# Full-size products of constants between the samples' small products, in one kernel of a decoder trunk

## The chip, the cores and the metric

The kernel runs on one core of one Trainium2 chip. The metric is the device time of a launch in microseconds. Before the change it is 3067.97 us, the median of three runs (3066.2 to 3071.03).

## What is computed

One layer of a hybrid decoder for two groups that share the weights: a prompt of 2048 tokens and 8 samples of 4 new tokens each, model width 1024. The layer is: RMS norm, one projection, three parallel head groups (A, windowed attention; B, dilated attention; C, an RWKV-7 recurrence of 6 heads of 64), output projection and residual, RMS norm, squared-ReLU MLP of width 4096 and residual, final norm. Everything is computed in f32, partly in sums of rounded halves.

The change lies in group C. Cut to what matters:

```
def wkv_scan(s0, r, w, k, v, kk, a):
    # S_t = S_{t-1} diag(w_t) + (S_{t-1}(-kk_t)) (kk_t*a_t)^T + v_t k_t^T ;  y_t = S_t r_t
    ...

def rwkv_mixer(zc, z_before, s0, w):
    z_prev = shifted by one token
    zs = zc + (z_prev - zc) * c_mu
    r, k, v, zw, za, zg = split(zs)
    decay = exp(-exp(-softplus(-(c_w0 + tanh(zw) @ c_w2)) - 0.5))
    a = sigmoid(c_a0 + za @ c_a2);  g = sigmoid(zg) @ c_g2
    kk = heads(k * c_k_k) / its norm over a head;  k = k * (1 + (a - 1) * c_k_a)
    y, s_fin = wkv_scan(s0, ...)
    y = norm of y over a head, * c_ln_w + c_ln_b, + sum(r * k * c_r_k) * v
    return y * g, s_fin
```

The prompt starts from a zero state, each sample from a state of its own (`state_c_wkv`).

## The kernel before

`decoder_trunk` (line 3366) calls the stages one after the other: `project`, `prompt_attention`, `rwkv` for the prompt (names `cp_...`, with the samples' attention as a side job), `rwkv` for the samples (`cs_...`), `out_project`, `mlp`. Each stage is a block of five engine programs with a barrier at its end. `project`, `out_project` and `mlp` are dense products of 128x128 weights.

`rwkv` (line 1543) writes the recurrence in chunks. For the prompt a segment is 256 tokens, in four chunks of 64, taken two at a time as a group. For the samples there is one segment, one group and one chunk, which holds all 32 tokens, four of each sample. All products are small: a product of one head takes 64 or 32 rows and columns of the 128x128 array, and the two heads of a pair lie in different halves of it. Each f32 product is two records in the trace.

The order of work is written out by hand. `walk` calls the same steps for each engine's program:

- `prepare(seg, i)`, `i` from 0 to 10: gates, decay, key norm. TensorE makes `w_pre`, `a_pre`, `g_pre`, `kksum` (i = 1 to 4), `kback` (i = 7, line 1722) and `bonus` (i = 9, line 1728). For the samples, `state_queries` stands here and there between them: the first state times `r`, 8 samples one after the other, products of 4 columns (line 1674).
- `levels_of`: the chunk's own matrices (`gab` and `m`, lines 1819 and 1826), their transposes `tok` (line 1841), one head of `state_rows` (line 1665), and then the inverse by doubling, in five levels for the prompt and one for the samples (`yl` line 1855, `dtt` line 1869).
- `hop`, prompt only: from chunk to chunk, `rhs`, `u` and then state and output `y` (lines 1778 to 1800), with a ScalarE copy after each. Those of the last group of the last segment have nothing left to stand between and follow one another.
- `special`, samples only: two state queries, the other five heads of `state_rows` (80 records), `rhs` (1881), `u` (1886), output (1892 and 1893).
- `finish(seg, i)`: mean (line 1743), variance (1749), its inverse spread back over the heads (1755). For the samples the twelve `update` products of the final state (line 1685, 512 columns) stand between these, one, one and ten; then VectorE adds and scales the state (2187, 2192) and SyncE stores it.

The engines wait for one another by counted semaphores: `E.done(product, name, seg)` on TensorE, `W_` where a result is needed. Each engine takes its instructions in the order written.

`keep_busy` (line 70) issues full-size products of the constant `hones` (128x128) into a bank that nobody reads. There are such products in both recurrences: 16 before the samples' first wait, some behind `prepare` 1 to 3, and 24 at the very end (`last_fill` 8); in the samples they go to `q[4]`, which `u` uses too. In the samples' stage ScalarE (`ahead.high`, lines 2499 and 2490) and VectorE (`ahead.low`, 2505 and 2495) also prepare the weights and the first two tiles of the output projection: ScalarE in `prepare` 6 to 9, ahead of `levels_of`; VectorE two pieces in `levels_of`, three in `special`, three in `finish` 9.

The results of `prepare` and `finish` go into `pb`, a view of four quarters of 256 columns, which is two banks of PSUM.

## Time and profile before

| | |
|---|---|
| median of three runs | 3067.97 us |
| the profiled execution | 3062.81 us |
| its span, first to last instruction | 3061.0 us |
| TensorE busy | 2921.0 us, 95% |
| VectorE, ScalarE, GpSimd busy | 2162.6, 944.7, 317.9 us |
| mean granted clock of TensorE | 0.981 |
| samples' recurrence, first instruction to the next stage's first product | 1418.67 to 1484.48 us |

The granted clock is the share of full speed (2.4 GHz) that TensorE was given; it has two levels here, 1.00 and 0.50. The table by stretches gives it for any stretch. In a timeline a row is a run of like instructions on one engine: start, time from the first's start to the last's end, engine, line, what is written and read, shape, count; in brackets the engine's idle time before it and what ended that. The end of a product is modelled, so the start of the next run says better how long one took.

### The profile page before, as it was taken

Reading aid. Unit: us, or ns where it says so; the run is one execution under the profiler, and the core shown is the slowest. Engines: PE = TensorE matmul, PEld = TensorE weight load, DVE = VectorE, ACT = ScalarE, POOL = GpSimd, SP = SyncE. Lnnn points to the kernel's source line nnn. Section 1 sums busy time; section 2 is a strip of 40 time slices with the busy share of each in tenths; the row PEclk is TensorE's granted clock in tenths of the full one; section 3 lists DMA queues with packets and bytes.
Section 4 is the critical chain, followed back from the end, with each engine's and each line's share of the span. In section 5 each row is a group of like instructions: output and inputs, shape, how many; then the busy total and the mean of one; then the engine's idle time right before and its main releaser. Section 6 shows DMA issues by size and latency. Waiting matters only on the chain. (4 is left out here: it accounts for less than half of the span.)

```text
span 3061.0 us, 65513 instructions
## 1 busy us (share of the span) xinstructions
PE 2921.0 (95%) x27757; PEld 2556.3 (84%) x27757; DVE 2162.6 (71%) x3708; ACT 944.7 (31%) x1414; POOL 317.9 (10%) x453
## 2 busy tenths in 40 slices
PE   8999999999888998898999999999999999999998
PEld 6899998566777877787787999999998888888886
DVE  4789885776566666654346999999997666666667
ACT  5533332655332333322133323323331111111013
POOL 0000000643232322330000000000000000000000
PEclk9999999999999999997899999999999999999999
DMA  7644443441222330002365533433436222212212
GB/s 230 206 128 164 139 139 110 143 122 56 73 94 89 105 110 28 23 8 83 115 189 183 185 124 137 173 123 135 166 126 243 70 70 70 84 56 84 70 56 112
DMA packets 182275, 353.48 MB, mean 115 GB/s; under 512 B 27776, under 2 KB 115968, under 8 KB 171488
## 3 DMA queue, kind: packets, MB, share of 16 engines
q1 hardware_dynamic: 181984, 349.29, 34.4%
q8 instruction: 220, 3.60, 0.5%
q14 instruction: 71, 0.58, 0.1%
HBM read 254.65 MB, written 94.60 MB: 114 GB/s over the span
## 5 line engine op out<-in xcount | busy, mean ns | idle before, releaser
L2960 PE MATMUL m_bank<-m_hh,m_wuh 128*128 128x348 f32 (+1 forms) x1344 | 431.5, 321 | 6.1 <-DVE m_wul L3196 4.6
L2961 PE MATMUL m_bank<-m_hl,m_wuh 128*128 128x348 f32 (+1 forms) x1344 | 429.4, 319 | 0.0
L3272 DVE TENSOR_TENSOR m_y_low<-m_y_low,m_bank 128x512 f32<-128x512 f32 x320 | 216.7, 686 | 152.5 <-PE m_bank L2962 149.8
L289 PE MATMUL p_bank<-p_hl,p_wh 128*128 128x348 f32 (+1 forms) x840 | 269.7, 321 | 0.0
L288 PE MATMUL p_bank<-p_hh,p_wh 128*128 128x348 f32 (+1 forms) x840 | 269.4, 321 | 0.0
L2960 PEld LDWEIGHTS m_bank<-m_hh,m_wuh 128*128 128x128 f32 x1344 | 253.0, 188 | 8.3 <-DVE m_wul L3196 5.2
L2961 PEld LDWEIGHTS m_bank<-m_hl,m_wuh 128*128 128x128 f32 x1344 | 253.4, 189 | 0.0
L2962 PE MATMUL m_bank<-m_hh,m_wsl 128*128 128x348 f32 (+1 forms) x768 | 246.3, 321 | 0.0
L2962 PE MATMUL m_bank<-m_wuh,m_wul 128*128 128x512 f32 x512 | 199.2, 389 | 0.0
L3214 DVE TENSOR_TENSOR m_stage<-m_stage,m_bank 128x348 f32<-128x348 f32 (+1 forms) x336 | 166.1, 512 | 45.6 <-PE m_bank L2962 40.6
L3272 DVE TENSOR_TENSOR m_mix<-m_mix,m_bank 128x512 f32<-128x512 f32 x192 | 130.1, 686 | 92.9 <-PE m_bank L2962 92.8
L2962 PE MATMUL m_bank<-m_hh,m_wul 128*128 128x348 f32 (+1 forms) x576 | 184.7, 321 | 0.0
L288 PEld LDWEIGHTS p_bank<-p_hh,p_wh 128*128 128x128 f32 x840 | 157.8, 188 | 0.1
L289 PEld LDWEIGHTS p_bank<-p_hl,p_wh 128*128 128x128 f32 x840 | 157.8, 188 | 0.0
L3066 ACT ACTIVATE m_wuh<-m_wur 128x1536 fp32r<-128x1536 f32 x47 | 70.1, 1491 | 279.4 <-PE m_bank L2962 279.4
L290 PE MATMUL p_bank<-p_hh,p_wsl 128*128 128x348 f32 (+1 forms) x480 | 153.9, 321 | 0.0
L558 DVE TENSOR_TENSOR p_stage<-p_stage,p_bank 128x348 f32<-128x348 f32 (+1 forms) x210 | 103.2, 512 | 62.5 <-PE p_bank L290 60.1
L2962 PEld LDWEIGHTS m_bank<-m_hh,m_wsl 128*128 128x128 f32 x768 | 144.7, 188 | 0.0
L2960 PE MATMUL m_bank<-m_wd,m_wsl 128*128 128x512 f32 x352 | 137.7, 391 | 0.0
L2961 PE MATMUL m_bank<-m_wd,m_wsl 128*128 128x512 f32 x352 | 137.0, 389 | 0.0
L2157 DVE TENSOR_TENSOR cp_Tm<-cp_Tm,cp_q 128x384 f32<-128x384 f32 x64 | 35.4, 554 | 142.7 <-PE cp_q L1865 71.8
L3070 ACT ACTIVATE m_wuh<-m_wsr 128x2048 fp32r<-128x2048 f32 x47 | 90.2, 1920 | 118.1 <-DVE m_wsr L3176 118.1
(477 smaller groups left out, 7194.4 us busy)
## 6 DMA issues: line engine op xcount, KB each, us to landing
m_wur<-w_up SPq DMA_DIRECT2D x48, 1024.0 KB, 5.3
p_war<-w_fm SPq DMA_DIRECT2D x30, 1024.0 KB, 6.3
m_wur<-uT SPq DMA_DIRECT2D x24, 1024.0 KB, 5.3
p_ring<-units SPq DMA_DIRECT2D x30, 768.0 KB, 5.8
uT<-m_stage SPq DMA_DIRECT2D x64, 348.0 KB, 4.9
out_projT<-p_stage SPq DMA_DIRECT2D x40, 348.0 KB, 6.7
cp_z<-out_projT SPq DMA_DIRECT2D x8, 1408.0 KB, 7.8
uT<-m_stage SPq DMA_DIRECT2D x32, 344.0 KB, 4.2
```

The lines of the kernel that those rows point to most:

```text
L288: pe.matmul(out, wh_, mh, start=first, stop=False)
L289: pe.matmul(out, wh_, ml, start=False, stop=False)
L290: return pe.matmul(out, wl_, mh, start=False, stop=last)
L558: dve.tensor_tensor(keep(q, to, n), keep(q, of, n), pbank(q, p, n), ALU.add).then_inc(joined, 1)
L2157: i = e.tensor_tensor(Tm[sl], Tm[sl], packed(1, sl), ALU.add)
L2960: pe.matmul(out, wh_, mh, start=first, stop=False)
L2961: pe.matmul(out, wh_, ml, start=False, stop=False)
L2962: return pe.matmul(out, wl_, mh, start=False, stop=last)
L3066: act.activation(wslot(wh[q % 2], A11, 3), wslot(wa[q % 3][0], 1, 3), ACT.Copy).then_inc(w_high, 1)
L3070: act.activation(wslot(wh[q % 2], S1, 4), ws[q % 2][0][:, :], ACT.Copy).then_inc(w_high, 1)
L3214: dve.tensor_tensor(keep(q, to, n)[:, 0, :], keep(q, of, n)[:, 0, :], pbank(q, p, n), ALU.add).then_inc(joined, 1)
L3272: dve.tensor_tensor(yh, yh, db[b % ND][:, :], ALU.add).then_inc(y_added, 1)
```

## The change

A bank of its own is made for the filling products of the samples: `pb` becomes 96 columns in a row in the first of its two banks, and `idle_bank` is in the second. `fill(n)` writes there in the samples' stage, and elsewhere into the bank `q[at]`. `last_fill` becomes a call of `fill`; its counts stay. New calls:

- samples: one behind each head of `state_rows` and of `state_queries`, one after every second update product but the last, two behind `gab`, one behind each `tok`, three behind `yl`, one behind `dtt`, three behind `rhs`, three behind `u`, two behind the output, and in `prepare` two behind `i = 4` and one behind `i = 7`;
- prompt: in the last group of the last segment two behind `u` of both chunks and two behind `rhs` of the second chunk, into `q[2]`.

Nothing waits for the new products; they stand in TensorE's order.

```
@@ -1598,7 +1598,8 @@
         S1 = s.sb(n_("S1"), [P, NP3, nb, HD])
         q = [s.ps(n_(f"q{i}"), [P, 512]) for i in range(6 if sample else 5)]
         pbanks = s.ps(n_("pb"), [P, 4, 256])
-        pb = pbanks[:, 0:NP3, 0:W]
+        pb = pbanks[:, 0, 0:NP3 * W].rearrange("p (a w) -> p a w", a=NP3) if sample else pbanks[:, 0:NP3, 0:W]
+        idle_bank = pbanks[:, 2, 0:P]
         c_in, z_in = own_.c_in, own_.z_in
         n_consts = own_.n_consts
         stored = s.sem(n_("stored"))
...
@@ -1656,6 +1657,10 @@
         def tensor_walk(e):
             W_ = lambda st, name, seg: st.wait(e, name, seg)
 
+            def fill(n, at=4):
+                if not isinstance(e, Rehearsal):
+                    keep_busy(e, idle_bank if sample else q[at][:, 0:P], hones[:, :], hones[:, :], n)
+
             def heads(n):
                 return [(p, h) for p in range(n) for h in range(2)]
 
...
@@ -1664,6 +1669,7 @@
                     for b in range(NB):
                         e.matmul(q[3][rows(h), p * HD:(p + 1) * HD], am[half(h), p, b, :], S0[half(h), 0, p, b, :],
                                  start=(p == 0 and b == 0), stop=False)
+                    fill(1)
 
             queries = heads(NP3)
 
...
@@ -1673,6 +1679,7 @@
                     for b in range(NB):
                         e.matmul(y_bank(half(h), p, NQ * b, NQ), S0[half(h), 0, p, b, :],
                                  ar_[0][half(h), p, 0, 1, NQ * b:NQ * (b + 1)], start=(p == 0 and b == 0), stop=False)
+                    fill(1)
 
             updates = [(name, t_, p, h) for t_, name in ((1, "vm"), (0, "um")) for p, h in heads(NP3)] if sample else []
 
...
@@ -1686,10 +1693,8 @@
                                   start=(name == "vm"), stop=(name == "um"))
                     if not updates:
                         E.done(mm, ("s", 0), 0)
-
-            def fill(n):
-                if not isinstance(e, Rehearsal):
-                    keep_busy(e, q[4][:, 0:P], hones[:, :], hones[:, :], n)
+                    elif len(updates) % 2 == 0:
+                        fill(1)
 
             def prepare(seg, i):
                 zs = zs_[seg % NPAR]
...
@@ -1730,11 +1735,7 @@
                     if sample:
                         state_queries(1)
                 if seg == 0:
-                    fill(({1: 3, 2: 3, 3: 2} if sample else {1: 6, 2: 6, 3: 5, 4: 16, 7: 3, 9: 7}).get(i, 0))
-
-            def last_fill(n):
-                if not isinstance(e, Rehearsal):
-                    keep_busy(e, q[4 if sample else 3][:, 0:P], hones[:, :], hones[:, :], n)
+                    fill(({1: 3, 2: 3, 3: 2, 4: 2, 7: 1} if sample else {1: 6, 2: 6, 3: 5, 4: 16, 7: 3, 9: 7}).get(i, 0))
 
             def finish(seg, i):
                 if i == 5:
...
@@ -1757,7 +1758,7 @@
                     E.done(mm, "vback", seg)
                     update(len(updates))
                 if seg == nseg - 1:
-                    last_fill(({8: 24} if sample else {5: 6, 7: 8, 8: 34}).get(i, 0))
+                    fill(({8: 24} if sample else {5: 6, 7: 8, 8: 34}).get(i, 0), 3)
 
             def previous(gc, seg):
 
...
@@ -1779,12 +1780,16 @@
                         mm = e.matmul(o, GB[rows(h), pg, c, p, 0, :], tok[rows(h), pg, 2, c * NP3 + p, :],
                                       start=False, stop=True)
                     E.done(mm, ("rhs", gc), seg)
+                    if seg == nseg - 1 and g == ngr - 1 and c:
+                        fill(2, 2)
                 elif k == "u":
                     W_(S, ("rhs", gc), seg); W_(V, ("tt", g, LL - 1), seg); W_(V, ("state", pc), ps)
                     for p, h in heads(NP3):
                         mm = e.matmul(q[4][rows(h), p * HD:(p + 1) * HD], Tt[rows(h), pg, c * NP3 + p, :],
                                       rh[rows(h), p, :], start=True, stop=True)
                     E.done(mm, ("u", gc), seg)
+                    if seg == nseg - 1 and g == ngr - 1:
+                        fill(2, 2)
                 else:
                     W_(S, ("u", gc), seg)
                     for p, h in heads(NP3):
...
@@ -1819,6 +1824,8 @@
                             mm = e.matmul(q[b][rows(h), p * 2 * C:(p + 1) * 2 * C], x[half(h), p, gc * C:(gc + 1) * C],
                                           ar[half(h), p, gc].rearrange("p a c -> p (a c)"), start=True, stop=True)
                     E.done(mm, ("gab", gc), seg)
+                    if sample:
+                        fill(2)
                     if c == 0:
                         for c1 in range(nc_):
                             for p, h in heads(NP3):
...
@@ -1840,6 +1847,8 @@
                             f = x[half(h), p + (6 if i == 2 else 0), (g * nc_ + c1) * C:(g * nc_ + c1 + 1) * C]
                             mm = e.matmul(q[b][rows(h), u * HD:(u + 1) * HD], f, id64[half(h), :], start=True, stop=True)
                     E.done(mm, ("tok", g, i), seg)
+                    if sample:
+                        fill(1)
                 if sample:
                     W_(V, "am", 0)
                     state_rows(heads(NP3)[0:1])
...
@@ -1854,6 +1863,8 @@
                     for u, h in units:
                         mm = e.matmul(q[0][rows(h), col(u)], ML[rows(h), l, u, :], Tm[rows(h), u, :], start=True, stop=True)
                     E.done(mm, ("yl", g, l), seg)
+                    if sample:
+                        fill(3)
                     between()
                     W_(S, ("ys", g, l), seg)
                     if l:
...
@@ -1869,6 +1880,8 @@
                         mm = e.matmul(q[2][rows(h), col(u)], Ys[rows(h), u, :], Tt[rows(h), pg, u, :],
                                       start=True, stop=True)
                     E.done(mm, ("dtt", g, l), seg)
+                    if sample:
+                        fill(1)
                     after(l)
 
             def special():
...
@@ -1881,17 +1894,20 @@
                     mm = e.matmul(q[3][rows(h), p * HD:(p + 1) * HD], GB[rows(h), 0, 0, p, 0, :], tok[rows(h), 0, 2, p, :],
                                   start=False, stop=(p == NP3 - 1))
                 E.done(mm, ("rhs", 0), 0)
+                fill(3)
                 W_(S, ("rhs", 0), 0); W_(V, ("tt", 0, LL - 1), 0)
                 for p, h in heads(NP3):
                     mm = e.matmul(q[4][rows(h), p * HD:(p + 1) * HD], Tt[rows(h), 0, p, :], rh[rows(h), p, :],
                                   start=True, stop=True)
                 E.done(mm, ("u", 0), 0)
+                fill(3)
                 W_(S, ("u", 0), 0)
                 for p, h in heads(NP3):
                     o = y_bank(half(h), p, 0, C)
                     e.matmul(o, uu[rows(h), p, :], GA[rows(h), 0, 0, p, 1, :], start=False, stop=False)
                     mm = e.matmul(o, tok[rows(h), 0, 2, p, :], GB[rows(h), 0, 0, p, 1, :], start=False, stop=(p == NP3 - 1))
                 E.done(mm, ("y", 0), 0)
+                fill(2)
 
             def extra(slot):
                 if side and not isinstance(e, Rehearsal):
...
@@ -2306,7 +2322,7 @@
         @block.tensor
         def _(pe):
             if sample:
-                keep_busy(pe, q[4][:, 0:P], hones[:, :], hones[:, :], 16)
+                keep_busy(pe, idle_bank, hones[:, :], hones[:, :], 16)
             pe.wait_ge(c_in, 16 * n_consts)
             if not sample:
                 keep_busy(pe, q[4][:, 0:P], hones[:, :], hones[:, :], 22)

```

## Rows read from the trace of the kernel before

**Rows 1.** the page, parts 1, 2 (granted clock in 40 slices) and 4 (chain)

```profile
PE 2921.0 (95%) x27757; PEld 2556.3 (84%) x27757; DVE 2162.6 (71%) x3708; ACT 944.7 (31%) x1414; POOL 317.9 (10%) x453
...
PEclk9999999999999999997899999999999999999999
...
PE 42%; DVE 2%; issue 0%; ACT 0%; DVEq 0%
```

**Rows 2.** by stretches: length, PE, PEld, DVE, ACT, POOL, clock, DMA, GB/s

```profile
1384.26:1386.64 2.38, 0.02 (x2) 0.00 (x1) 2.25 (x4) 0.33 (x1) 0.00 (x0) 1.00 0.00 0
...
1387.20:1400.80 13.60, 11.39 (x181) 10.38 (x177) 1.43 (x4) 1.65 (x5) 0.00 (x0) 0.50 0.06 22
...
1400.80:1431.56 30.76, 25.82 (x225) 23.79 (x224) 13.50 (x43) 7.78 (x19) 1.26 (x3) 1.00 0.46 166
...
1431.56:1479.30 47.74, 43.24 (x366) 31.73 (x366) 24.91 (x54) 13.01 (x24) 2.28 (x6) 0.50 0.07 18
```

**Rows 3.** the same table, state and output products of the prompt at either clock

```profile
1382.14:1384.26 2.12, 2.12 (x68) 2.00 (x64) 1.81 (x5) 0.00 (x0) 0.00 (x0) 1.00 0.03 8
...
1396.90:1400.90 4.00, 3.73 (x60) 3.54 (x60) 0.71 (x2) 0.21 (x1) 0.00 (x0) 0.51 0.00 0
```

**Rows 4.** timeline, TensorE, state queries and norm product of the samples

```profile
1429.09 1.82 PE L1674 MATMUL cs_q<-cs_ar,p_ring 64*64 64x4 f32 x32 [0.77 <-DVE cs_ar L2008]
...
1430.84 0.86 PE L1722 MATMUL cs_pb<-cs_ksum,rw_hback 96*128 96x32 f32 x6
```

**Rows 5.** table by stretches, the filling products (line 72) alone: PE, PEld, clock

```profile
1409.20:1416.90 7.70, 7.70 (x68) 7.56 (x67) 1.00 0.22 62
...
1423.50:1428.20 4.70, 2.56 (x16) 2.02 (x16) 1.00 1.02 414
...
1476.68:1479.30 2.62, 2.62 (x12) 2.62 (x13) 0.50 0.00 0
```

**Rows 6.** timeline, TensorE, from the level product to the products of rhs

```profile
1444.26 0.53 PE L1855 MATMUL cs_q<-cs_Tm,cs_ML 32*32 32x32 f32 x12 [1.65 <-ACT cs_tok L1965]
...
1445.46 0.53 PE L1869 MATMUL cs_q<-cs_Tt,cs_Ys 32*32 32x32 f32 x12 [0.66 <-ACT cs_Ys L1970]
...
1445.92 3.17 PE L1674 MATMUL cs_q<-cs_ar,p_ring 64*64 64x4 f32 x32
...
1449.02 7.06 PE L1665 MATMUL cs_q<-p_ring,cs_am 64*32 64x64 f32 x80
...
1456.01 0.85 PE L1881 MATMUL cs_q<-cs_tok,cs_GB 32*32 32x64 f32 x12
```

**Rows 7.** timeline, all engines, from the mean product to the output projection

```profile
1461.06 1.49 PE L1743 MATMUL cs_pb<-cs_y,rw_hmean 128*128 128x32 f32 x6 [0.35 <-ACT cs_y L1987]
...
1468.06 0.25 DVE L2100 TENSOR_TENSOR cs_yc<-cs_yc,cs_pb 128x96 f32<-128x96 f32 x1 [2.63 <-PE cs_pb L1755]
...
1469.56 3.49 DVE L2505 TENSOR_TENSOR p_wl<-p_wr,p_wh 128x1024 fp32r<-128x1024 f32 x3
...
1476.80 1.88 DVE L2187 TENSOR_TENSOR cs_S<-p_ring,cs_q 128x512 f32<-128x512 f32 x3 [3.74 <-PE cs_q L1685]
...
1478.71 1.90 DVE L2192 TENSOR_TENSOR cs_S<-cs_S,cs_De 128x512 f32<-128x512 f32 x3
...
1484.48 0.47 PE L2725 MATMUL m_bank<-p_wh,p_mh 128*128 128x512 f32 x1 [0.92 <-PEq L1561]
```

**Rows 8.** timeline, last hops of the prompt

```profile
1388.27 0.91 PE L1785 MATMUL cp_q<-cp_rh,cp_Tt 64*64 64x64 f32 x12 [0.42 <-ACT cp_rh L1951]
...
1393.37 0.33 ACT L1957 ACTIVATE cp_y<-cp_q 128x192 f32<-128x192 f32 x1 [3.82 <-PE cp_q L1800]
```

**Rows 9.** timeline, ScalarE, samples

```profile
1434.37 1.06 ACT L2490 ACTIVATE p_mh<-p_mix 128x1024 fp32r<-128x1024 f32 x1 [3.48 <-DMA p_mix<-mixT]
...
1437.22 5.77 ACT L2499 ACTIVATE p_wh<-p_wr 128x1024 fp32r<-128x1024 f32 x6
...
1442.90 1.99 ACT L1965 ACTIVATE cs_tok<-cs_q 32x192 f32<-32x192 f32 x6
```

More of the change, by code:

```diff
@@ L1600, in rwkv @@
         pbanks = s.ps(n_("pb"), [P, 4, 256])
-        pb = pbanks[:, 0:NP3, 0:W]
+        pb = pbanks[:, 0, 0:NP3 * W].rearrange("p (a w) -> p a w", a=NP3) if sample else pbanks[:, 0:NP3, 0:W]
+        idle_bank = pbanks[:, 2, 0:P]
         c_in, z_in = own_.c_in, own_.z_in
@@ L1657, in tensor_walk, with fill @@
             W_ = lambda st, name, seg: st.wait(e, name, seg)
+            def fill(n, at=4):
+                if not isinstance(e, Rehearsal):
+                    keep_busy(e, idle_bank if sample else q[at][:, 0:P], hones[:, :], hones[:, :], n)
             def heads(n):
@@ L1666, in state_rows @@
                                  start=(p == 0 and b == 0), stop=False)
+                    fill(1)
             queries = heads(NP3)
@@ L1675, in state_queries @@
                                  ar_[0][half(h), p, 0, 1, NQ * b:NQ * (b + 1)], start=(p == 0 and b == 0), stop=False)
+                    fill(1)
             updates = [(name, t_, p, h) for t_, name in ((1, "vm"), (0, "um")) for p, h in heads(NP3)] if sample else []
@@ L1688, in update @@
                         E.done(mm, ("s", 0), 0)
-            def fill(n):
-                if not isinstance(e, Rehearsal):
-                    keep_busy(e, q[4][:, 0:P], hones[:, :], hones[:, :], n)
+                    elif len(updates) % 2 == 0:
+                        fill(1)
             def prepare(seg, i):
@@ L1732, in prepare @@
                 if seg == 0:
-                    fill(({1: 3, 2: 3, 3: 2} if sample else {1: 6, 2: 6, 3: 5, 4: 16, 7: 3, 9: 7}).get(i, 0))
-            def last_fill(n):
-                if not isinstance(e, Rehearsal):
-                    keep_busy(e, q[4 if sample else 3][:, 0:P], hones[:, :], hones[:, :], n)
+                    fill(({1: 3, 2: 3, 3: 2, 4: 2, 7: 1} if sample else {1: 6, 2: 6, 3: 5, 4: 16, 7: 3, 9: 7}).get(i, 0))
             def finish(seg, i):
@@ L1759, in finish @@
                 if seg == nseg - 1:
-                    last_fill(({8: 24} if sample else {5: 6, 7: 8, 8: 34}).get(i, 0))
+                    fill(({8: 24} if sample else {5: 6, 7: 8, 8: 34}).get(i, 0), 3)
             def previous(gc, seg):
@@ L1781, in hop @@
                     E.done(mm, ("rhs", gc), seg)
+                    if seg == nseg - 1 and g == ngr - 1 and c:
+                        fill(2, 2)
                 elif k == "u":
@@ L1787, in hop @@
                     E.done(mm, ("u", gc), seg)
+                    if seg == nseg - 1 and g == ngr - 1:
+                        fill(2, 2)
                 else:
@@ L1821, in levels_of @@
                     E.done(mm, ("gab", gc), seg)
+                    if sample:
+                        fill(2)
                     if c == 0:
@@ L1842, in levels_of @@
                     E.done(mm, ("tok", g, i), seg)
+                    if sample:
+                        fill(1)
                 if sample:
@@ L1856, in levels_of @@
                     E.done(mm, ("yl", g, l), seg)
+                    if sample:
+                        fill(3)
                     between()
@@ L1871, in levels_of @@
                     E.done(mm, ("dtt", g, l), seg)
+                    if sample:
+                        fill(1)
                     after(l)
@@ L1883, in special @@
                 E.done(mm, ("rhs", 0), 0)
+                fill(3)
                 W_(S, ("rhs", 0), 0); W_(V, ("tt", 0, LL - 1), 0)
@@ L1888, in special @@
                 E.done(mm, ("u", 0), 0)
+                fill(3)
                 W_(S, ("u", 0), 0)
@@ L1894, in special @@
                 E.done(mm, ("y", 0), 0)
+                fill(2)
             def extra(slot):
@@ L2308, in _ @@
             if sample:
-                keep_busy(pe, q[4][:, 0:P], hones[:, :], hones[:, :], 16)
+                keep_busy(pe, idle_bank, hones[:, :], hones[:, :], 16)
             pe.wait_ge(c_in, 16 * n_consts)
```

## The prediction

> **What bounds the kernel now.** The page comes first: TensorE is busy 95% of the span, and the chain that ended last runs over TensorE's dense products [rows 1]. So what starts those products earlier shortens the whole. The PEclk row of the page has one dip, at slices 18 and 19. The table by stretches shows what it is [rows 2]: TensorE's clock is at its lower level (0.50, that is 1.2 of 2.4 GHz) from 1387.2 to 1400.8 us and from 1431.56 to 1479.3 us, and at 1.00 between and after. The first of them lies in the last hops of the prompt's recurrence, the second is nearly the whole samples' recurrence. Each is a chain through TensorE and the engines that copy its results, and at its end a barrier starts the output projection. A microsecond saved on these chains is a microsecond of the kernel.
>
> Before the first fall TensorE sat idle for 2.4 us; the clock came back at 1400.8 after 3.7 us of small products without a pause, before any full-size one [rows 2, 3]. Before the second fall it ran 32 products of 4 columns and six of 32 columns, one after the other and none of 128x128x128 [rows 4]: busy, and the clock still fell. It stayed low for 47.7 us with TensorE busy 43.2 of them, and came back 2.6 us after the closing run of full-size products began [rows 2, 5]. From 1423.5 to 1428.2, with 16 full-size records (16 x 0.113 = 1.8 us) between products of 32 columns, it had stayed up [rows 5]. So small products alone don't hold the clock in the samples' part, and a few full-size ones among them do. That is the ground on which I expect the change to work; what remains is how long it is up, and what the added products cost.
>
> **The price of an added product.** `fill(1)` is two records of 128x128. At the full clock 68 records take 7.70 us, 0.113 each, so 0.23 us for one fill; at the low clock 12 take 2.62 us, 0.44 us for one fill [rows 5]. The samples get 37: 3 in `prepare`, 6 behind state queries, 2+3+3+1 in `levels_of`, 6 behind state rows, 3+3+2 in `special`, 5 between updates. That is 8.4 us at the full clock and 16 us at the low one. The prompt's tail gets 6.
>
> What the clock gives back is in rows at both levels. From the start of 32 query products to the start of what follows is 1.75 us at the full clock and 3.10 us at the low one, a ratio of 1.8 [rows 4, 6]; six of 128x32 take 0.86 us and 1.49 us [rows 4, 7]; 60 of the prompt's state and output products take 3.73 us low, and 68 records of that stretch 2.12 us full [rows 3].
>
> **Part 1, the prompt's last hops.** Six fills, two each behind `u` of both chunks and `rhs` of the second. ScalarE's copies leave TensorE idle 0.42 us there [rows 8]; two fills are 0.45 us at full, 0.87 at low clock, so hidden at full and 0.3 to 0.45 us late each at low. The fall at 1387.2 comes before the first of them and stays. In the closing run it was back 2.6 us after the first full-size record [rows 5]; I take about 1390.6 for it here, instead of 1400.8. Saved: 1.1 of the first output group (3.8 us, as the second one from 1396.9 [rows 3], copied from 1393.37 on [rows 8]; 1 us of it is still slow), 1.6 of the second, 0.75 of the second chunk's `rhs` and `u`; less 0.3 for the first fills. That is 3.2 us; where the clock comes back later it is less, and if not at all it is +1.2. I take **-2.5**. The tail behind it shifts whole: store, state store and barrier follow one another.
>
> **Part 2, samples up to 1444.26.** Nine fills lie between the norm product at 1430.84 and the level's first product, and nothing is gained or lost by them: the level waits for ScalarE's copies of `tok`, and ScalarE is in its weight casts until 1442.9, nine in a row since the DMA of the mix landed at 1434.37 [rows 9]. TensorE already waits 1.65 us there [rows 6]. At the full clock its work of about 9 us becomes 5, and 2 us of fills go in: **0**. It will then sit idle about 4 us before 1444.26, longer than the 2.4 us of the first fall, with no fill in it: here I expect the clock to fall once more. If it is low before, nine fills (3.9 us) meet 1.65 us of wait: up to +2.3.
>
> **Part 3, 1444.26 to 1456.01.** Three fills follow the level product, in ScalarE's 0.66 us [rows 6]: 0.68 at full (hidden), 1.31 at low (+0.6). From 1445.46 to 1456.01 TensorE runs without a pause: 12 products, 32 queries, 80 state rows, 10.55 us at the low clock [rows 6]. At full that is 10.55 / 1.8 = 5.9, and the eight fills add 1.8: 7.7, so -2.85. At low they add 3.5: +3.5. The four fills at the head (three, one) are about 1.7 us of low-clock full-size work, the densest here; I expect the clock back about 3 us after 1444.3. Half the gain at the start is lost: **-1.0**.
>
> **Part 4, 1456.01 to 1461.06**, `rhs`, `u`, output [rows 6, 7]: 36 packed products with ScalarE's copies between. The products are about 3.1 of 5.05 us; with latencies that don't shrink I take 0.9 off. The fills behind `rhs` and `u` (0.68 each at full) fit in waits of 0.75; the two behind the output (0.45) stand before the mean product, which waits only 0.35: +0.1. **-0.8**. At low: +0.6, +0.6, +0.5.
>
> **Part 5, 1461.06 to 1476.80** [rows 7]: mean, one update, variance, one update, norm product, ten updates; TensorE is the bound, since VectorE waits 2.6 us for the norm product and 3.7 us for the updates. The products take 15.7 us and at full 7.9 to 8.3; five fills add 1.1. VectorE's way from the norm product to its sum is 0.9 + 1.5 + 3.49 (casts), about 5.9 us, as long as TensorE's new 6.0, so no more is to be had: 9.4 for 15.74, **-6.3**. At low the fills add 2.2.
>
> **Part 6.** Afterwards nothing: VectorE's two passes take 3.8 us, the state's store and the barrier 3.9 us to 1484.48 [rows 7]; the 24 closing products (5.4 us at full) end before it. The bank for the fills and the closer layout of `pb` change no size: 0.
>
> The sum is -2.5 + 0 - 1.0 - 0.8 - 6.3 = **-10.6 us**. The profiled execution took 3062.81 us, 5.2 us less than the median of the three runs, 3067.97; the difference of two levels should carry over, so 3067.97 - 10.6 = 3057.4, **3057 us**.
>
> **A rule against the change.** Small products of different row groups overlap, and a full-size one covers all row groups. Were each fill on the path (16 in parts 3 to 5 that no wait hides) to make its neighbours wait for its full length, 0.274 - 0.113 = 0.16 us apiece, 2.6 us would be lost. Against it: 68 full-size records follow at 0.113 us though each lasts 0.274 [rows 5], so a load does not wait for the product ahead even in the same row groups. The Trainium skill ("TensorE: Matmul & The Clock Gate", Part 3, The mechanism) says that a weight load overlaps products in flight only when its row group differs. By that rule the sum would be near -8; by the row, -10.6.
>
> **The rivals.**
> - A (likeliest), as summed: 3057 us.
> - B: the clock that fell in the wait before 1444.26 isn't back until the dense fills behind `rhs` and `u`. For: eight fills are strung thinly over 10 us there. Against: the four at its head. Part 3 is then +3.5 + 0.6, part 4 +0.6, part 5 -6.3, prompt -2.5: -4.1, **3064**.
> - C: no fall at all in the wait: -12.5, **3055.5**. Against: 4 us of idle.
> - D: fills serialise: -8, **3060**.
> - E: TensorE's gain doesn't reach the end, or as much is lost in part 2 as won in part 5: within 2 us of **3068**. Against it: the first product of the projection waits for the barrier alone.
> - F, the other side: the fills are too thin, and the clock stays low from 1431 to the closing run. It decides where the fills neither keep the clock up nor bring it back. Then +2.3 + 4.1 + 1.7 + 2.2 and +1.2 in the prompt's tail: +11.5, **3079.5**. For it: they are 8.4 us of work in 37, thinner than the 1.8 in 4.7 us that were seen to hold. Against it: they stand among products that work too, and in the prompt's hops products of 64x64 alone brought the clock back [rows 3].
>
> **Chances:** A 0.45, B 0.25, C 0.08, D 0.09, E 0.07, F 0.06. A, C and D are more than 0.2% (6.1 us, about what a measurement of this kernel tells from no change) faster: 0.62; B and E are the same: 0.32; F slower: 0.06. A alone spans 3053 to 3061 (the prompt's 0.7 either way, part 3 from -2.85 to +1, scatter of the runs). With C, D and B the range is 3051 to 3067; what is left out is most of E, and F.
>
> **What would show it.** The table by stretches should show 1.00 from the norm product near 1430 to the wait before the level, a low piece of 3 to 4 us around it, and 1.00 to the end; PE's products in part 5 at half their length, five pairs of updates in 4.3 us for 8.6; the low stretch in the prompt's hops 3 to 7 us for 13.6; ScalarE's casts and the `tok` copies at the same distance from the DMA. The prediction is wrong if the low clock lasts through the state rows (B), if the time from the level to the projection shrinks by less than 6 us, or if the records behind a fill start late (D).

## The result, and the profile after

After the change the kernel takes 3088.21 us, the median of six runs (3080.84 to 3093.06), against 3067.09 us for the kernel before beside it (six runs, 3056.79 to 3072.91). The ratio is 1.0070, with an interval from 1.0057 to 1.0084: slower by 0.7%, where 3057 us was forecast and 3067 was the upper end. The profiled execution took 3080.84 us, its span 3079.1 us, 18 us longer than that of before.

The page first: busy time by engine, and the granted clock in 40 slices.

```profile
PE 2945.9 (96%) x27843; PEld 2575.2 (84%) x27843; DVE 2162.8 (70%) x3708; ACT 945.1 (31%) x1414; POOL 316.9 (10%) x453
...
PEclk9999999999999999996799999999999999999999
```

TensorE is busy for 25 us more than before, and the dip in PEclk is still there and deeper, 6 and 7 tenths for 7 and 8 [rows 1]. The table by stretches over the places of [rows 2] (length, PE, PEld, DVE, ACT, POOL, clock, DMA, GB/s):

```profile
1380.90:1384.30 3.40, 3.40 (x47) 3.08 (x45) 0.47 (x2) 0.33 (x1) 0.00 (x0) 0.50 0.00 0
1384.30:1415.00 30.70, 26.02 (x292) 23.81 (x289) 11.76 (x32) 4.91 (x12) 1.22 (x3) 1.00 0.25 86
1415.00:1496.90 81.90, 81.90 (x514) 62.17 (x514) 28.60 (x70) 16.99 (x34) 2.36 (x7) 0.50 0.12 41
```

The first row is the prompt's last hops: the low piece is 3.4 us there, not 13.7. The last row is the samples: the clock is at 0.50 (1.2 GHz) for 81.9 us instead of 47.7, and TensorE was busy for every one of them. In the kernel before it had been busy 43.24 of 47.74 us [rows 2]. So the added products did what they were put there for, they filled every gap, and the clock neither stayed up nor came back. It returned in the closing run of 48 full-size records, where it had returned in the kernel before too.

The samples' stage, from its first filling product to the first product of the output projection, cut at the same places in both traces:

| part | before, us | after, us | forecast | measured |
|---|---|---|---|---|
| start to the level product | 25.55 | 35.95 | 0 | +10.4 |
| level product to `rhs` | 11.74 | 21.10 | -1.0 | +9.4 |
| `rhs` to the mean product | 5.05 | 7.18 | -0.8 | +2.1 |
| mean product to the state's sum | 15.73 | 19.68 | -6.3 | +3.9 |
| state's sum to the projection | 7.69 | 8.23 | 0 | +0.5 |
| whole stage | 65.77 | 92.13 | -8.1 | +26.4 |

(the last row is worked out from unrounded times). The prompt's tail, from the end of ScalarE's third last copy of `y` to the end of its last, takes 13.79 us instead of 16.62. The rest of the span is +2.1 us behind the stage and 7.5 us less ahead of the tail, where nothing was changed and short pieces of low clock (3 to 17 us) come and go from one execution to the next (inter2 and inter2_b below, one kernel, differ in them too). Stage and tail together are +23.5 us, the two medians 21 us apart.

Now the second row of that table, part 3 of the prediction, line by line. TensorE in the changed kernel, from the level product on:

```profile
1444.31 0.53 PE L1864 MATMUL cs_q<-cs_Tm,cs_ML 32*32 32x32 f32 x12
1444.77 1.65 PE L72 MATMUL cs_pb<-rw_hones 128*128 128x128 f32 x6
1446.35 0.53 PE L1880 MATMUL cs_q<-cs_Tt,cs_Ys 32*32 32x32 f32 x12
...
1452.58 1.91 PE L1670 MATMUL cs_q<-p_ring,cs_am 64*32 64x64 f32 x16
1454.42 0.79 PE L72 MATMUL cs_pb<-rw_hones 128*128 128x128 f32 x2
1455.14 1.91 PE L1670 MATMUL cs_q<-p_ring,cs_am 64*32 64x64 f32 x16
...
1465.41 0.85 PE L1894 MATMUL cs_q<-cs_tok,cs_GB 32*32 32x64 f32 x12
...
1482.36 1.97 PE L1692 MATMUL cs_q<-cs_vm,cs_tok 32*64 32x512 f32 x4
1484.27 0.80 PE L72 MATMUL cs_pb<-rw_hones 128*128 128x128 f32 x2
1484.99 1.97 PE L1692 MATMUL cs_q<-cs_um,cs_tok 32*64 32x512 f32 x4
...
1492.14 7.90 PE L72 MATMUL cs_pb<-rw_hones 128*128 128x128 f32 x48
1500.49 0.47 PE L2741 MATMUL m_bank<-p_wh,p_mh 128*128 128x512 f32 x1 [0.45 <-PEq L1561]
```

Read start to start. A head of `state_rows` and its fill take 1455.14 - 1452.58 = 2.56 us; the same 16 records took 6.99 / 5 = 1.40 us [rows 6]. One fill costs 1.16 us there, where I had put 0.44. Of that 0.72 is from the fill's start to the next head's, and 0.44 is what the 16 records themselves lost. Alone they take 1.84 us; in the kernel before four records of each head start within 0.01 us of one of the head before it, and with a fill between the heads none does. Behind a head of queries it is +0.97. The ten updates behind the norm product take 12.40 us with four fills between them, and 8.73 without: +0.92 each.

ScalarE in the same kernel, which answers to [rows 9]:

```profile
1426.91 5.77 ACT L2515 ACTIVATE p_wh<-p_wr 128x1024 fp32r<-128x1024 f32 x6
1438.12 0.65 ACT L1981 ACTIVATE cs_tok<-cs_q 32x192 f32<-32x192 f32 x2 [5.45 <-PE cs_q L1848]
1439.63 0.65 ACT L1981 ACTIVATE cs_tok<-cs_q 32x192 f32<-32x192 f32 x2 [0.85 <-PE cs_q L1848]
1441.14 0.65 ACT L1981 ACTIVATE cs_tok<-cs_q 32x192 f32<-32x192 f32 x2 [0.85 <-PE cs_q L1848]
```

The casts end 24.3 us after the stage's start, as before (1442.9 - 1418.7 = 24.2). But the products of `tok`, which had been ready when ScalarE came to copy them, now keep it waiting 5.45 us and twice 0.85 us. The cover under which nine fills were costed at nothing was 1.65 us thick, and it was gone.

### The profile page after: what moved, and what is told of

It reads as the page before. It is cut to its first block and busy times, and to the rows that moved or that the text cites. A ratio compares the mean times of both kernels' runs of the same rounds, so it can differ in the third digit from the quotient of the medians.

```text
span 3079.1 us, 65685 instructions
## 1 busy us (share of the span) xinstructions
PE 2945.9 (96%) x27843; PEld 2575.2 (84%) x27843; DVE 2162.8 (70%) x3708; ACT 945.1 (31%) x1414; POOL 316.9 (10%) x453
```

## Experiments

Two theories were open when the first four kernels were written: that each change between a small and a full-size product costs TensorE most of its overlap (rival D, larger), and that the sparse fills don't hold the clock (rival F); and against them that the new layout of `pb` or the prompt's fills were to blame. All times are against the kernel before, run beside them. None of these kernels leaves computation of the reference out; they differ in added products of constants, or in order. "Stage", "tail" and the parts are those of the table above. `dense`, `half2`, `lump` and `inter` were run once each: what is read from them is their profile, not the total.

**p_only: the prompt's six fills alone**

```
 prompt, last group of the last segment: fill(2, 2) behind u, u, rhs    kept
-samples: all 37 new fills, idle_bank, pb
```

> The kernel before with the six fills of the prompt's last hops alone; the samples' part as before. Theory 1 (the prompt's share of the prediction holds, the loss is all in the samples): the low stretch that begins in the last hops lasts 3 to 7 us instead of 13.7, from the stretch's first rhs to the store of the prompt's state 2 to 4 us are saved, the whole is 2 to 4 us faster (ratio 0.9987 to 0.9993). Theory 2 (fills among packed products lose everywhere): 1 to 2 us slower. Rival: no difference that can be measured, because the prompt's tail is covered by the store of the samples' attention.

Measured: 3065.98 us, ratio 1.0007 (0.9996 to 1.0019, 12 runs). Tail 14.98 us with 6.8 us at the low clock, stage 65.89 us, as before (65.77). So the samples' part of the change makes the whole loss; of the 2 to 4 us that were expected from the prompt's fills the total shows nothing. The clock in its samples' stage fell 7.0 us after the start, where that of the kernel after fell 6.7 us after it; but with nothing added it was back at 1.00 at +27.4 us, for 3.4 us.

That fall is a finding of its own. The samples' stage of this kernel is the one of before, and 7.0 us after its start, at 1431.28, TensorE is between the same 16 full-size records beside which the prediction had read that the clock holds. Two runs of six of them, on either side of the fall:

```profile
1429.90 0.94 PE L72 MATMUL cs_q<-rw_hones 128*128 128x128 f32 x6
...
1431.74 1.65 PE L72 MATMUL cs_q<-rw_hones 128*128 128x128 f32 x6
```

**w_only: new bank and layout, prompt's fills, and only 11 of the samples' 37**

```
-                    fill(1)        # state_rows, state_queries
-                    elif len(updates) % 2 == 0: fill(1)
-  gab 2, tok 1 each, dtt 1, output 2, prepare 7: 1
   yl 3, rhs 3, u 3, prepare 4: 2   # kept
```

> The changed kernel with only those fills of the samples that stand where TensorE waits anyway: 2 behind i = 4, 3 behind yl, 3 behind rhs, 3 behind u; none behind queries, state rows, gab, tok, dtt, output, updates (26 of the 37 go). Theory 1 (a fill costs because it stands between packed products that TensorE is bound by): 18 to 24 of the 26 us that the samples' stage lost come back, the stage is 66 to 70 us from its first product to the projection's first (64.5 to 65.8 before, 92.1 after); the clock stays low from about 1431 to the closing run. Rival (the loss comes from the earlier fall of the clock near 1415, or from the new layout of the bank): the stage stays above 80 us.

Measured: 3066.8 us, ratio 1.0007 (0.9993 to 1.0020, 12 runs); stage 69.47 us. Taking away 26 fills gives back 22.7 of the 26.4 us, about 2 of them perhaps because the clock fell later, 13.0 us after the start. The bank and the layout of `pb` are therefore not the cause. TensorE in this kernel:

```profile
1441.72 1.65 PE L72 MATMUL cs_pb<-rw_hones 128*128 128x128 f32 x6
1443.30 0.53 PE L1872 MATMUL cs_q<-cs_Tt,cs_Ys 32*32 32x32 f32 x12
1443.76 3.17 PE L1679 MATMUL cs_q<-cs_ar,p_ring 64*64 64x4 f32 x32
1446.86 7.06 PE L1670 MATMUL cs_q<-p_ring,cs_am 64*32 64x64 f32 x80
1453.85 0.85 PE L1884 MATMUL cs_q<-cs_tok,cs_GB 32*32 32x64 f32 x12
1454.63 1.65 PE L72 MATMUL cs_pb<-rw_hones 128*128 128x128 f32 x6
```

The 80 state rows are back at 7.06 us and the queries at 3.17, to the hundredth what [rows 6] show, and with twice six full-size records within 15 us the clock stays low (51.2 us in all).

**lump: the same number of fills as after, but behind all heads of a call instead of behind each**

```
             def state_rows(some):
                 for p, h in some:
                     for b in range(NB): e.matmul(...)
-                    fill(1)
+                fill(len(some))
```

> The changed kernel with the same number of fills, but those of state rows in one run behind the last head of each call (1 and 5) instead of one behind each. After: 16 records and a fill take 2.56 us at the low clock, five of them 12.8 us. Theory 1 (what costs is the change of shape and the lost overlap of neighbouring heads, not the fill's own 0.44 us): the 80 records take 7.0 us again and the five fills 2.2 to 2.5 us: 9.3 us, 3.5 us less. Rival (the fills' own length): 12.8 us again, or 12.4.

Measured: 3074.04 us (one run), stage 82.53 us against after's 92.13, of which 3.4 us are the state rows:

```profile
1455.69 7.06 PE L1670 MATMUL cs_q<-p_ring,cs_am 64*32 64x64 f32 x80
1462.68 2.50 PE L72 MATMUL cs_pb<-rw_hones 128*128 128x128 f32 x10
1465.11 0.85 PE L1894 MATMUL cs_q<-cs_tok,cs_GB 32*32 32x64 f32 x12
```

From the first row to the last record of the five fills 9.42 us, where after has 12.83 (1465.41 - 1452.58) for the same 90 records. Five fills in one run cost 2.43 us, 0.49 each, close to the 0.44 of [rows 5]; apart they cost 5.84. The cost is that of the changes, two for each fill that stands alone, and of the overlap of neighbouring heads that goes with them. The clock also came back, 54.6 us after the stage's start, just behind this run of ten, for 6.8 us; so this difference of the whole stage holds both effects, the state rows' part only the first (its clock is low in both).

**dense: eight fills behind each head of state rows**

```
                     for b in range(NB): e.matmul(q[3]..., am..., S0...)
-                    fill(1)
+                    fill(8)
```

> The changed kernel with eight fills instead of one behind each head of state rows. Theory 1 (the clock comes back only in a stretch where full-size products are most of the time): it is at 1.00 after the second or third head of special, and the remaining heads show the price of a fill at the full clock: 16 state rows plus eight fills in 0.9 to 1.1 us plus 8 x 0.23 = 1.8 us plus a fixed part of 0.2 to 0.4. Rival (the clock isn't given back in this stage before the closing run whatever is filled in): 0.50 throughout, a head takes 1.7 + 8 x 0.44 + 0.3 = 5.5 us.

Measured: 3087.5 us (one run), stage 86.55 us: with 42 fills more than after it is 5.6 us shorter. By stretches:

```profile
1428.90:1459.60 30.70, 30.70 (x226) 27.44 (x225) 10.92 (x39) 14.32 (x25) 2.32 (x6) 0.50 0.29 96
1459.60:1486.90 27.30, 27.30 (x315) 23.37 (x314) 8.30 (x13) 2.59 (x9) 0.00 (x0) 1.00 0.00 1
1486.90:1504.00 17.10, 17.10 (x51) 8.09 (x51) 8.66 (x15) 0.00 (x0) 0.00 (x0) 0.50 0.02 4
```

and TensorE around the return of the clock and after it:

```profile
1456.04 3.73 PE L72 MATMUL cs_pb<-rw_hones 128*128 128x128 f32 x16
...
1461.60 1.09 PE L1680 MATMUL cs_q<-cs_ar,p_ring 64*64 64x4 f32 x16
1462.62 0.49 PE L72 MATMUL cs_pb<-rw_hones 128*128 128x128 f32 x2
1463.04 1.09 PE L1680 MATMUL cs_q<-cs_ar,p_ring 64*64 64x4 f32 x16
...
1464.48 1.08 PE L1670 MATMUL cs_q<-p_ring,cs_am 64*32 64x64 f32 x16
1465.49 2.05 PE L72 MATMUL cs_pb<-rw_hones 128*128 128x128 f32 x16
1467.47 1.08 PE L1670 MATMUL cs_q<-p_ring,cs_am 64*32 64x64 f32 x16
```

The clock came back at the end of the first run of 16 full-size records (3.7 us of them), stayed as long as such runs stood between the heads, and fell again at 1486.9, in the mean and update part, where one fill stood behind two updates. TensorE was busy all the time in all three stretches. Of rival F's two readings, that fills hold the clock nowhere and that these ones are too sparse, this one profile speaks for the second: the clock stayed up for 27.3 us, in p_only for 3.4. That the run of 16 also brought it back isn't shown, for in p_only it came back 10.8 us sooner after the stage's start with nothing added. And it is no bargain: a head of state rows with its run takes 2.99 us at the full clock, twice the 1.40 us of the kernel before at the low one. The queries give the price of a lone fill at the full clock as well: 1463.04 - 1461.60 = 1.44 us, where 16 such records took 1.75 / 2 = 0.87 [rows 4]. That is +0.57 for one fill, where I had 0.23.

**half and half2: a small neighbour in place of the full-size one, in the other half of the array**

Every product of `state_rows` and `state_queries` is followed by one constant product in the other half's rows and columns, 96 in all: 64x64 in `half`; in `half2` 64x32 behind state rows, the tile form that they have, and 64x64 behind queries, again theirs. The prompt's fills are kept, all other new ones are out.

```
                     for b in range(NB):
                         e.matmul(q[3][rows(h), ...], am[half(h), p, b, :], S0[...], ...)
+                        other(h)        # half: 64x64;   half2: other(h, C), 64x32
```

> The kernel of p_only, with the new banks, and in the samples 96 added products of 64x64 with 64 columns, one behind each state query and each state row, in the other half of the array's rows and columns than their neighbours; no full-size fills added. Theory 1 (what costs is that a full-size product shares row groups with its neighbours): the 80 state rows of special take 7 us as before or up to 8.6 (the overlap of neighbouring heads, 12 of 16 records each, goes), and the clock may come back there, since the array is nearly twice as busy; the whole is within 3 us of the kernel before, or faster. Theory 2 (every added product costs its own columns, wherever it lies): 96 x 0.21 us, 15 to 20 us slower.

> As half, but the product behind each state row is 64x32 with 64 columns in the other half, the shape of its neighbours. In half each pair of state row and 64x64 product took 0.747 us at the low clock, while behind the state queries (64x64 like the added ones) the added products fitted in between and cost nothing. Theory 1 (a change of the tile's shape makes TensorE run empty, the row group by itself does not matter): the pair takes 0.21 us, as two records of one head do, the 80 records of special 8.6 us instead of 30, the samples' stage 66 to 70 us. Theory 2 (any added product behind a state row has to wait for it): 0.5 us or more a pair, the stage above 80 us.

Measured: half 3092.45 us, ratio 1.0094 (1.0079 to 1.0110, 4 runs), stage 95.24 us; half2 3063.03 us (one run), stage 64.24 us. TensorE in the state rows of half:

```profile
1455.42 0.42 PE L1670 MATMUL cs_q<-p_ring,cs_am 64*32 64x64 f32 x2
1455.77 0.47 PE L72 MATMUL cs_pb<-rw_hones 64*64 64x64 f32 x2
1456.17 0.42 PE L1670 MATMUL cs_q<-p_ring,cs_am 64*32 64x64 f32 x2
```

and of half2, also at the low clock:

```profile
1452.07 0.31 PE L1671 MATMUL cs_q<-p_ring,cs_am 64*32 64x64 f32 x1
1452.09 0.31 PE L72 MATMUL cs_pb<-rw_hones 64*32 64x64 f32 x1
1452.18 0.31 PE L1671 MATMUL cs_q<-p_ring,cs_am 64*32 64x64 f32 x1
```

In half a product and its neighbour (two records each) take 0.75 us: the two records of one form start 0.11 us apart (the neighbour's 0.16), and the first of the next form 0.24 us after the last of the one before. In half2 the records interleave, one each in 0.107 us, 0.21 us for the same two products, against 6.99 / 40 = 0.175 for the row product alone [rows 6]. Only the neighbour's columns differ, 32 for 64; its rows, its half of the array and the moving operand are alike. In half itself the 64x64 neighbours behind 64x64 queries interleave too (32 records of queries with 32 of neighbours in 3.6 us at the low clock, against 3.1 for the queries alone [rows 6]). So what costs is a change of tile form between neighbours, although they lie in different halves: about 0.27 us a change here, (0.75 - 0.21) / 2, the lost overlap included. The 29 us by which half is slower were in neither expectation (within 3 us, or 15 to 20). half2 came out as its first theory had it (stage 66 to 70 us forecast), and it also shows that 96 added small products do no harm. The clock fell 7.6 us after the stage's start, as in p_only, and was low for 41 us of the stage, where p_only had 51; from one profile of each I conclude nothing on that.

**inter, inter2, inter2_b: no fills; the two heads of a pair take turns**

If overlap is what counts, the kernel before leaves some: it does eight products of one head, then eight of the other, all in one half.

```
-                for p, h in some:
-                    for b in range(NB):
+                for p, b, h in [(p, b, h) for p in ... for b in range(NB) for h in range(2)]:
```

The same in `state_queries`, so heads go by pairs (two in `prepare` 9, none behind `gab`, two heads of rows ahead of the level). inter2 and inter2_b (one kernel, run on two occasions) also put the first two updates together behind the mean product. All keep the prompt's six fills.

> p_only with the two heads of a pair interleaved in state queries and state rows (record by record they lie in different rows and columns of the array), queries 2, 2, 2 and rows 2 and 4 heads per call; no fill added or moved in the samples. Theory 1 (products of one shape in different quarters run side by side, and the heads one after the other were what held the samples' stage): 16 records of a pair's rows take 0.9 us at the low clock instead of 1.3 to 1.7; from the level to rhs 11.7 us become 7 to 8; the stage is 61 to 62 us; the clock may also come back in that stretch. Rival (weight loads are the bound at 0.107 us each): no change, 65.8 us.

> inter, and the first two update products (512 columns, one half each) side by side behind the mean instead of one behind mean and one behind variance. Theory 1: another 1.7 us at the low clock, the stretch from mean to the state's sum is 14.0 us instead of 15.7; the stage is 59.5 to 60.5 us; the whole 5 to 7 us faster than before (ratio 0.9977 to 0.9984), with the prompt's fills up to 9. Rival (VectorE's casts are the bound as soon as TensorE gets shorter there): stage 61 to 62 us, ratio above 0.9985.

> inter2 once more, beside the other two on one chip: 0.9984 of the kernel before again, 0.9975 to 0.9992. Rival (the first measurement was luck of the chip): the interval takes in 1.

Measured: inter 3052.98 us (one run), stage 58.39 us. inter2 3058.21 us, ratio 0.9984 (0.9969 to 0.9999, 12 runs), stage 57.92; inter2_b 3053.3 us, ratio 0.9963 (0.9950 to 0.9975, 5 runs), stage 57.86. TensorE in inter2_b:

```profile
1443.82 1.10 PE L1672 MATMUL cs_q<-cs_ar,p_ring 64*64 64x4 f32 x32
1444.85 1.98 PE L1664 MATMUL cs_q<-p_ring,cs_am 64*32 64x64 f32 x64
1446.76 0.53 PE L1881 MATMUL cs_q<-cs_tok,cs_GB 32*32 32x64 f32 x12
```

and its stretches, and then TensorE in inter:

```profile
1422.60:1443.10 20.50, 17.63 (x220) 16.53 (x219) 9.65 (x41) 14.43 (x26) 2.27 (x6) 0.50 0.51 165
1443.10:1449.90 6.80, 4.88 (x152) 4.41 (x153) 6.72 (x10) 1.63 (x6) 0.00 (x0) 1.00 0.02 5
1449.90:1470.40 20.50, 19.38 (x77) 10.81 (x75) 12.43 (x22) 0.82 (x3) 0.00 (x0) 0.50 0.03 10
```

```profile
1439.75 1.92 PE L1664 MATMUL cs_q<-p_ring,cs_am 64*32 64x64 f32 x32
1441.60 0.53 PE L1855 MATMUL cs_q<-cs_Tm,cs_ML 32*32 32x32 f32 x12
```

Both stages are shorter than expected (61 to 62 us for inter, 59.5 to 60.5 for inter2), and the ratio of inter2_b is better than its range. 64 state rows take 1.91 us, 0.030 a record, for 0.087 before. Two things are in that: the interleaving (in inter, above, 32 records take 1.85 us, 0.058 each, while its clock is low until 1442.3) and the clock, which is up at 1.00 for 6.8 us from 27.2 us after the stage's start on, behind 15 us of small products. In p_only it was up at nearly the same distance, but its level product stood 1.1 us later and the clock fell 3.4 us after it had come, at the start of the long row of state products; here the rows and what follows them fit in. From level product to `rhs` it is 4.4 us instead of 11.7. How these 7.3 us divide between taking turns and the clock isn't measured; at inter's 0.058 a record the turns alone would take 2.3 us off 80 state rows, an estimate. inter2 beats both kernels: 0.2 to 0.4% faster than the one before in two comparisons, and 1% faster than the one after.

**inter2_np: inter2 without the prompt's fills**

```
-                    if seg == nseg - 1 and g == ngr - 1 and c: fill(2, 2)
-                    if seg == nseg - 1 and g == ngr - 1: fill(2, 2)
```

> inter2 without the six fills of the prompt's last hops. Theory 1 (they save 1.6 to 2.9 us there, as the traces with them show from the copy of the third last output to the last: 13.7 to 15.0 us for 16.6): 1.5 to 3 us slower than inter2, that stretch 16 to 17 us. Rival (they save nothing that reaches the end, as the timing of p_only left open): the same as inter2 or faster.

Measured: 3057.64 us, ratio 0.9980 (0.9971 to 0.9989, 11 runs); tail 14.23 us with 6.8 us at the low clock. inter2 beside the same runs of before had 13.78 and 3.4. Over all profiles the low piece in the hops was 3.4 us seven times and 6.8 four times with the fills, 6.8 once and 13.7 once without. The expectation (that stretch 16 to 17 us without fills) failed. On the same occasion inter2_b, with the fills, was 4.3 us faster (3053.3, five runs, for 3057.64), and the intervals just overlap; on the other occasion inter2 had 0.9984, no better than inter2_np. The two profiles differ by 0.45 us in the tail and 1.4 us in the stage. Whether the prompt's fills are worth anything stays open; the 2.8 us that the two profiles of the change show can't be put down to them.

**inter3: inter2 with fills where they should hurt least**

```
+  fill(3) behind rhs, fill(3) behind u, fill(2) behind every second update
```

> inter2 with a bank for the fills, three fills behind rhs and u of the samples (in ScalarE's waits) and two behind every second update. In inter and inter2 the clock was at 1.00 from about 27 to 34 us after the stage's first product and fell again near the mean. Theory 1 (fills work where they keep up a clock that is up, in waits or between long products): it stays up to the end of the updates, from mean to the state's sum 10 to 11.5 us instead of 14.7 to 15.7, stage 54 to 56 us, 2 to 4 us faster than inter2. Rival (two fills between updates do not hold the clock, as one did not in dense): at the low clock five times 1.2 us more, stage 63 to 65 us, slower than inter2 by 5 us.

Measured: 3059.03 us, ratio 0.9988 (0.9977 to 0.9999, 11 runs); stage 62.30 us against 57.9. The clock fell 37.4 us after the start, 3.4 us later than without the fills, and stayed low for the updates:

```profile
1458.63 1.97 PE L1684 MATMUL cs_q<-cs_vm,cs_tok 32*64 32x512 f32 x4
1460.53 1.22 PE L72 MATMUL cs_pb<-rw_hones 128*128 128x128 f32 x4
1461.68 1.97 PE L1684 MATMUL cs_q<-cs_vm,cs_tok 32*64 32x512 f32 x4
```

3.05 us for a pair of updates with its two fills; the ten updates with four times two fills take 14.12 us, and 8.73 without, 1.35 us for each two. From the mean product to the state's sum it is 19.82 us, against 14.69 without. The rival of the expectation held (62.3 us, with 63 to 65 forecast): the sparse fills kept the clock up for 3.4 us more at the most, and through the ten updates it was low.

## Why the prediction was wrong

**What it rested on.** "So small products alone don't hold the clock in the samples' part, and a few full-size ones among them do." The second half is the step that failed. It came from one stretch of 4.7 us, 1423.5 to 1428.2, in which the clock had been up and 16 full-size records stood; what came before that stretch (32 full-size records at the start) was not weighed, and one place where two things go together is no proof that one holds the other. In p_only, with the same products in the same order, the clock fell in the middle of that stretch. In the changed kernel fills of two to six records stood between nearly all groups of small products for 77 us, and the clock was low throughout. The other half of the sentence doesn't say enough either: in p_only and the inter kernels the clock came back behind some 15 us of small products alone, and fell again 3.4 us (p_only) or 6.8 us (inter2_b) later.

**The price of an added product** was the second failure. By itself it would not have taken the time out of the range: at the full clock the 16 fills on the path, each 0.34 us dearer than the prediction had them, are 5.4 us, an estimate from the queries of dense. The clock by itself would have: rival F, at the prediction's own price of a fill, is 3079.5. At the low clock the price more than doubled the loss: F has +10.3 for the samples' stage, and +26.4 was measured. 0.44 us at the low clock and 0.23 at the full one were read from rows of like products [rows 5]; such a row says nothing of a change of form. Measured: +1.16 behind state rows, +0.97 behind queries, +0.92 behind updates, +0.84 for three behind `yl` beyond ScalarE's wait; +0.57 behind queries at the full clock. Where the product behind a fill is itself nearly or quite full-size, the price was about right: from the last output product to the update behind the mean product (128x128) it is 2.62 us with two fills, and 2.19 with none and ScalarE's wait of 0.35; from the update ahead of `vback` (96x128) to the one behind it, 3.74 with one fill and 3.31 without.

**The rule against the change.** I set the rule aside for "a load does not wait for the product ahead even in the same row groups" and gave the case where fills serialise 0.09. The queries of dense show two and a half times my price at the full clock, 0.57 for 0.23, and the prediction had kept the rule's 0.16 apiece out of its sum. The Trainium skill ("TensorE: Matmul & The Clock Gate", Part 3, The mechanism) ties the overlap to a difference of row group; the trace agrees that a full-size product among small ones loses it, but half and half2 show that a difference of row group isn't enough: with the row group different in both, a neighbour of another form cost 0.57 us and one of the same form 0.04.

**Part 1**, the prompt's hops: -2.5 forecast, -2.8 in the profiles, by the steps named (the clock back 3.4 us after its fall). But this was luck in part: inter2_np, with no fills there, has a tail of 14.23 us, which is 2.4 of the 2.8 us, and the total of p_only shows no gain.

**Part 2**: 0 was forecast with "up to +2.3" if the clock were low; it was +10.4. The term: the fills up to the level product, and a clock that fell at +6.7 us where it had fallen at +12.8, so that TensorE's own work there was slow too; the cover was 1.65 us. The prediction counts nine fills there; the part has thirteen, for four of the 37 stand ahead of the norm product and were put into no part's sum. p_only, with the early fall and no fills, takes 27.58 us in this part, lump, with the same fills and the same fall as after, 35.8. By that the early fall is about 2 of the 10.4 us, and the thirteen fills about 8.4, 0.65 us each.

**Part 3**: the low branch of the forecast was +3.5 + 0.6 = +4.1; measured +9.4 = 0.84 (three at `yl`) + 0.73 (`dtt`) + 1.94 (two at queries) + 5.84 (five at state rows). **Part 4**: low branch +1.7, measured +2.1. **Part 5**: low branch +2.2, measured +3.9: four at 0.92 and one at 0.43 are 4.1, and the update behind the mean product came 0.17 us sooner. Rival F had the clock right, and its sum, +11.5, was short by the price of a fill. Rivals D and F came together, and I had weighed each by itself (0.09 and 0.06), at the full clock for D and at the row's price for F.

**Part 6** held but for 0.5 us.

## What to carry to other kernels

A filler product must have the tile form of its neighbours, or stand in a run; a lone full-size product (two records) between small ones cost 2.1 to 2.6 times what it takes in a run, and the 37 of the change held no clock. Before filling gaps of a chain of small products, put neighbours of the same form in the two halves of the array in turns: with nothing added to the stage, and the clock back at 1.00 for 6.8 us of it, that took 8 us off 66 us. And when a trace shows a clock level beside some activity, look for a stretch with the activity and the other level before building on it.

## What the runs showed of the hardware that was not expected

- TensorE busy 81.9 of 81.9 us, with full-size records between nearly all groups of its small ones, stayed at 1.2 GHz (after). With 17.6 of 20.5 us busy, and nothing but small products in the last 15 of them, it went back to 2.4 GHz (inter2_b).
- A change of tile form between neighbours in different halves of the array costs about 0.27 us at the low clock, the lost overlap included (0.75 us for two products in half, for 0.21 with like forms in half2).
- Two records of one form that lie in the two halves run in the time of one: in half2 such a pair starts every 0.107 us at the low clock, and in the kernel before records of one head alone follow at 0.107 us too (its mean of 0.087 [rows 6] has the overlap between heads in it).
- In the samples' stage the clock fell 6.6 to 7.6 us after the start in ten of the thirteen profiles, filled or not, and 11.5 to 13.0 us after it in three (before, w_only, inter2_np). What decides between them wasn't found; inter2 and inter2_b, the same kernel, agree to 0.1 us in the first fall and the return.
- The sparse full-size fills went with a later return, not an earlier one. Of the ten profiles with the early fall the seven without new full-size products ahead of the level (p_only, half, half2, inter, inter2, inter2_b, inter3) had the clock back after 20.5 us; with them it took 30.7 (dense, behind its run of 16), 47.8 (lump) and 81.9 us (after). That the fills caused it isn't shown; before, with the later fall and no new fills, was low for 47.8 us.
